# Feed-forward outputs with one 512-column product for the high and low activations

## What is computed

```python
def _swiglu(h, w_in, w_out):
    a, b = jnp.split(h @ w_in, 2, axis=-1)
    return (jax.nn.silu(a) * b) @ w_out

for layer in range(DEPTH):                      # DEPTH = 2
    x = x + 0.5 * _swiglu(_rmsnorm(x, ffn_norm[layer, 0]), ffn_w_in[layer, 0], ffn_w_out[layer, 0])
    ...                                         # hybrid mixer (layer 0), stick-breaking attention (layer 1)
    x = x + 0.5 * _swiglu(_rmsnorm(x, ffn_norm[layer, 1]), ffn_w_in[layer, 1], ffn_w_out[layer, 1])
```

## Time and profile before

| | |
|---|---|
| time, median of 3 runs | 2232.5 us (2226.9, 2232.5, 2237.2) |
| profiled execution: its own time | 2229.42 us |
| profiled execution: span of the trace | 2227.7 us |
| granted clock, mean over the span | 0.986 of full speed |
| TensorE busy with matmuls | 2143.9 us (96%) |
| VectorE busy | 1384.0 us (62%) |
| ScalarE busy | 847.6 us (38%) |
| L2002, L2003, L2004 (output stages) | 704 matmuls each, 287, 283 and 283 ns mean |
| L2499, L2500 (merged form, second block) | 256 matmuls each, 394 and 277 ns |
| L1210 and L1213 (evacuation) | 32 each, 419 and 426 ns |
| output stages, from first to last matmul start | about 157, 503, 710 and 1058 us on, some 70 us each |

### The profile page before, as it was taken

One profiled execution on the slowest core, in us unless ns is written; L12 is line 12 of the kernel. 1 busy time (PEld: TensorE's weight loads), 2 busy tenths in 40 slices (PEclk: granted clock), 3 DMA queues, 4 the chain that ended last, 5 costly groups with the idle time before them and its releaser, 6 DMA issues.

```text
span 2227.7 us, 43246 instructions
## 1 busy us (share of the span) xinstructions
PE 2143.9 (96%) x17274; PEld 1878.6 (84%) x17274; DVE 1384.0 (62%) x2303; ACT 847.6 (38%) x1336; POOL 28.9 (1%) x58
## 2 busy tenths in 40 slices
PE   7999999999999999899999999999999999999998
PEld 7999878999999998899986676788888876559987
DVE  6666657666666677766664556674355355657854
ACT  4444634444444444444531444421111233334332
POOL 0000000000000000000000000000000000000000
PEclk9999999999999999999999999999999999989999
DMA  7665424665666552466641110222222222003544
GB/s 269 245 228 185 167 75 175 241 238 183 240 237 224 198 182 99 167 229 246 226 176 38 39 39 20 102 76 94 94 95 94 95 95 95 1 19 120 182 174 147
DMA packets 50229, 325.73 MB, mean 146 GB/s; under 512 B 5328, under 2 KB 8656, under 8 KB 16976
## 3 DMA queue, kind: packets, MB, share of 16 engines
q1 hardware_dynamic: 42480, 266.62, 33.7%
q0 software_dynamic: 7648, 57.71, 6.9%
HBM read 323.26 MB, written 1.05 MB: 146 GB/s over the span
## 4 chain that ended last, share of the span: by engine, by line
PE 84%; DVE 9%; ACT 4%; issue 2%; DMA 0%; ACTq 0%; DVEq 0%; SPq 0%
PE psum L1914 17%; PE psum L1915 16%; PE psum L1916 16%; PE psum L2002 4%; PE psum L2003 4%; PE psum L2004 4%; PE psum L2499 3%; DVE w_lo L1062 2%; PE psum L2023 2%; PE psum L2338 2%; PE psum L2500 1%; ACT scratch L866 1%; ACT w_hi L620 1%; PE psum L2358 1%; PE psum L2321 1%
## 5 line engine op out<-in xcount | busy, mean ns | idle before, releaser
L1062 DVE TENSOR_TENSOR w_lo<-raw,w_hi 128x1024 fp32r<-128x1024 f32 (+1 forms) x534 | 590.2, 1146 | 229.3 <-ACT w_hi L620 215.3
L620 ACT ACTIVATE w_hi<-raw 128x1024 fp32r<-128x1024 f32 (+1 forms) x542 | 514.6, 991 | 572.3 <-PE psum L1916 351.6
L1914 PE MATMUL psum<-h_hi,w_hi 128*128 128x256 f32 (+1 forms) x2136 | 641.6, 300 | 12.8 <-DVE w_lo L1062 6.4
L1915 PE MATMUL psum<-h_lo,w_hi 128*128 128x256 f32 (+1 forms) x2136 | 633.5, 297 | 0.0
L1916 PE MATMUL psum<-h_hi,w_lo 128*128 128x256 f32 (+1 forms) x2136 | 633.1, 296 | 0.0
L1914 PEld LDWEIGHTS psum<-h_hi,w_hi 128*128 128x128 f32 x2136 | 410.1, 192 | 32.7 <-issue 12.8
L1916 PEld LDWEIGHTS psum<-h_hi,w_lo 128*128 128x128 f32 x2136 | 410.5, 192 | 10.1
L1915 PEld LDWEIGHTS psum<-h_lo,w_hi 128*128 128x128 f32 x2136 | 410.5, 192 | 9.8
L2002 PE MATMUL psum<-g_both,w_hi 128*128 128x256 f32 x704 | 202.2, 287 | 3.6 <-DVE w_lo L1062 3.6
L2003 PE MATMUL psum<-g_both,w_hi 128*128 128x256 f32 x704 | 199.3, 283 | 0.0
L2004 PE MATMUL psum<-g_both,w_lo 128*128 128x256 f32 x704 | 199.3, 283 | 0.0
(11 more groups left out here) (349 smaller groups left out, 3250.1 us busy)
## 6 DMA issues: line engine op xcount, KB each, us to landing
raw<-in_weights SPq DMA_DIRECT2D x207, 1024.0 KB, 4.8
raw_ada<-in_ada POOLq DMA_DIRECT2D x48, 1024.0 KB, 6.9
raw<-in_weights SPq DMA_DIRECT2D x64, 704.0 KB, 4.1
arena<-in_rpb POOLq DMA_DIRECT2D x1, 2048.0 KB, 10.9
arena<-in_fox_c POOLq DMA_DIRECT2D x1, 1696.0 KB, 9.2
const_region<-in_latent_c POOLq DMA_DIRECT2D x1, 1394.0 KB, 6.8
const_region<-in_even_c POOLq DMA_DIRECT2D x1, 1360.0 KB, 8.1
x_res<-in_x_lat SPq DMA_DIRECT2D x4, 256.0 KB, 7.1
```

Of the source, the lines that this page charges most:

```text
L620: nc.scalar.activation(wh[s][:, a], raw[s][:, a], ACT.Copy).then_inc(hi_ready, 1)
L1062: V.tensor_tensor(wl[s][:, a], raw[s][:, a], wh[s][:, a].bitcast(F32), ALU.subtract).then_inc(lo_ready, 1)
L1914: mm(out, sh, mh, start=n == 0, stop=False)
L1915: mm(out, sh, ml, start=False, stop=False)
```

## The change

In the output stages of the four feed-forward parts, the two matmuls of weight high become one of 512 columns: its moving operand is `g_both[:, :, g0:g0 + T]`, 256 high and then 256 low activations. Its result fills the whole bank: columns 0 to 255 get weight high times high, columns 256 to 511 weight high times low. The matmul of weight low adds to the first 256 columns only. The sum of the two halves is then formed by VectorE: a copy of the second half into `n_add`, an addition of the first half, and only then the scaling, now from `n_add` to `n_add`.

```diff
@@ -1207,9 +1207,11 @@
                     if q % 2:
                         c = q // 2
                         dve.wait_ge(gemm_done, pos.e + q + 1)
-                        V.scalar_tensor_tensor(n_add, psum[:, (pos.u + c) % 2, 0:T], 0.25, n_inv, ALU.mult,
-                                               ALU.mult).then_inc(bank_free, 1)
+                        b = (pos.u + c) % 2
+                        step(V.tensor_copy(n_add, psum[:, b, T:TJ]))
+                        V.tensor_tensor(n_add, psum[:, b, 0:T], n_add, ALU.add).then_inc(bank_free, 1)
                         freed(pos.u + c)
+                        step(V.scalar_tensor_tensor(n_add, n_add, 0.25, n_inv, ALU.mult, ALU.mult))
                         V.tensor_tensor(x[:, c, 0:T], x[:, c, 0:T], n_add, ALU.add).then_inc(x_new, 1)
                         dve.wait_ge(x_new, pos.n("xn", 1))
                         if gain:
@@ -1993,15 +1995,14 @@
                     half = j % 2
                     if half == 0:
                         bank(pos.u + 2 * i + j // 2)
-                    out = psum[:, (pos.u + j // 2) % 2, 0:T]
+                    out = psum[:, (pos.u + j // 2) % 2, :]
                     for k in range(FH):
                         a, g0 = k * P, (half * FH + k) * T
                         first, last = half == 0 and k == 0, half == 1 and k == FH - 1
                         if isinstance(i, int) and j == 1:
                             pe.wait_ge(g_ready, gb + FH + k + 1)
-                        mm(out, wh[s][:, a:a + P], gh[:, g0:g0 + T], start=first, stop=False)
-                        mm(out, wh[s][:, a:a + P], gl[:, g0:g0 + T], start=False, stop=False)
-                        ins = mm(out, wl[s][:, a:a + P], gh[:, g0:g0 + T], start=False, stop=last)
+                        mm(out, wh[s][:, a:a + P], g_both[:, :, g0:g0 + T], start=first, stop=False)
+                        ins = mm(out[:, 0:T], wl[s][:, a:a + P], gh[:, g0:g0 + T], start=False, stop=last)
                     ins.then_inc(gemm_done, 1)
```

## The result

| | before | with the change |
|---|---|---|
| time, median | 2237.1 us (5 runs, 2226.9 to 2239.1) | 2256.0 us (5 runs, 2248.6 to 2258.8) |
| profiled execution, span | 2227.7 us | 2254.6 us |
| granted clock, mean | 0.986 | 0.985 |
| VectorE busy | 1384.0 us | 1411.5 us |

The kernel became slower: ratio 1.0084, 95% interval 1.0063 to 1.0105, which is +19 us (14 to 23). The forecast was 2250 (2239 to 2259), or +18 by its sum. In a second set of runs the ratio was 1.0094 (1.0073 to 1.0115).

What follows compares the result with a forecast made beforehand. The prediction took TensorE and VectorE to be in balance in the output stages, each bounding one panel of a pair. 15.3 + 1.0 + 1.7 = +18.0 on 2229.4 gave 2247.4, plus 3.1 for the median: 2250 us (2239 to 2259).

Steps and rivals of the forecast that it cites:

- What bounds the kernel: Output stages: TensorE and VectorE in balance, each bounding one panel of a pair; TensorE stands still 0.15 us awaiting `w_lo`.
- Part 1, the merged matmul: TensorE, output stages: a block takes 0.3475 us against 0.36, saving 12.5 ns a block, 8.8 us over 704 blocks.
- Part 2, VectorE: VectorE's evacuation in the output stages: copy and addition are new, scaling costs nothing more; each evacuation grows by 0.92 us.
- d: Growth of one VectorE evacuation: 0.46 + 0.46 = 0.92 us, with ends of 0.79 and 1.0.
- Part 3, f = 0 to 2: First three output stages: pairs of panels go from 8.16 to 8.94 us; +5.1 us a stage, +15.3 for three.
- Part 4, f = 3: Fourth output stage, with looser pairs: stalls of 3.04 us, less 2.06 from shorter panels, +1.0 us.
- Part 5, behind the stages: Behind the output stages: later last evacuations cost +0.8 us after f = 0, nothing after f = 1 and 2, +0.9 after f = 3.
- The sum: Whole kernel: 15.3 + 1.0 + 1.7 = +18.0 us.
- The first (addition hidden, saving in full): Change from even to odd panel: VectorE's addition is hidden, TensorE's saving counts in full, 2224 us; chance 0.05.
- The second (part of the stall absorbed): VectorE's evacuation: copy and addition overlap or waits are free, growth near 0.6 us, +9, 2241 us; chance 0.1.
- The third (the clock): First three output stages: TensorE's standstills lower its clock; +8 us, so 2258, or +25 to +30; chance 0.08.
- The fourth (a second wait): Pairs of panels: transfers or ScalarE end behind VectorE, 0.2 to 0.4 us in each of 21, 2254 to 2258; chance 0.07.

Runs made afterwards that it cites:

- the order alone: Kernel before, with only `w_lo` of the next odd panel made earlier and ScalarE's square later, in the first three output stages: 2229.0 us, ratio 0.9986.
- the merged matmul alone: The change, but VectorE evacuates with one instruction as before and leaves out the bank's second half: 2231.5 us, ratio 0.9983 to before.
- VectorE's part alone: Kernel before with its three 256-column matmuls, plus two extra VectorE instructions of the change's kinds in each evacuation: 2259.5 us, ratio 1.0109.
- the change in three stages with the new order: The change for f = 0, 1 and 2 only, with `w_lo` ahead of the evacuation's rest; f = 3 as before: 2224.2 us, ratio 0.9965 to before.
- the copy made twice: The change with VectorE's copy of the bank's second half executed twice: 2272.2 us, ratio 1.0165 to before.
- the change with `w_lo` ahead: The change, with the next odd panel's `w_lo` made right after copy and addition, and ScalarE's square later: 2231.3 us, ratio 0.9985 to before.

## Why the prediction was right, and where its terms were off

**What bounds the kernel.** Right, and shown: the order alone brings all periods to 7.92. The shortening of TensorE's stream alone (the merged matmul alone) gave next to nothing, and VectorE's part alone gave the whole loss. The reading that foretold it was the 0.15 us of standing still between two panels, in a stage where TensorE is busy for 98.6% of the time.

**Part 1, the merged matmul.** The form is right, the size was taken from one stage and varies. In the profiled trace of the change a block steps by 0.3515 to 0.3535, in that of the change in three stages with the new order by 0.347. So the saving in the trace of the change was about 7.5 ns a block in place of 12.5. That accounts for the period of 9.02 in place of 8.94: 0.06 us on the odd panel, and some hundredths in reading.

**Part 2, VectorE.** d = 0.92 was right: steps of 0.46, a copy from PSUM at 425 ns, where copies within SBUF take 288. The choice between the two rows of copies was the one that counted.

**Part 3, f = 0 to 2.** Foretold +5.1 each from the start, or +5.24 between the first and last evacuation; measured +5.7 to +5.8. The step of 0.353 explains 0.4 of the missing half microsecond.

**Part 4, f = 3.** Foretold +1.0 (+1.1 between first and last evacuation), measured +2.2. The term was too small by half. The stalls with their restarts add up to about what was listed, 3.2 in place of 3.04, but not each in its place: panel 3 cost 0.64 where 0.24 was listed, and panel 13 cost 0.54 where 0.70 was; panel 5 cost nothing, as foretold. The shorter block gave back less (7.5 ns instead of 12.5 over 15 panels: 0.8 us), and the last evacuation came later. In the profile it starts 0.67 after the last matmul's start, where it was 0.32: the larger `w_lo` of the next stage and the work for the second block's norm end only at 1152.1, right ahead of it, which I had not followed.

**Part 5, behind the stages.** +0.8, 0, 0 and +0.9 were foretold and measured. What was missing is the clock: the same +0.9, with the late evacuation, stretched a standstill of 1.9 us to 3.2, and the granted clock fell behind it: +2.8 in one trace and +1.5 in the other, at some distance from every edited line. No term of the sum stood for it.

**The sum.** 18.0 foretold. The two measurements give 19 and 21, and the stretches that the change touches 24 in the profiled execution with the clock's part and 21 without. The median of 2256 lies inside the range, in its upper half. That +18 and +19 lie so close is partly luck. In the profile the terms that were foretold came to 21, three too few in parts 3 and 4, and the clock's part on top was in no term; the runs (+14 to +23) can't tell 18 from 21.

**The rivals.** The first (addition hidden, saving in full) fell with VectorE's part alone and with the merged matmul alone. The second (part of the stall absorbed) fell with the copy made twice. The third (the clock) did not happen where I put it: the clock is 1.00 in all output stages, even with standstills of 1.5 us in every pair. It did happen behind the last stage. Its price was put too high there: where the clock is 0.50 a 256-column matmul starts 0.213 us after the last one instead of 0.12, so a panel of before would take 3.1 us more, not 3.8. The fourth (a second wait) has no sign in the periods: with VectorE's part alone they are 9.08, the sum without any other wait.

**What stays open.** Why the same merged form steps by 0.347 in some stages and 0.353 in others, even within one execution (f = 0 and 1 of the change with `w_lo` ahead) or in two executions of one kernel (the last feed-forward part). Why the clock fell after a standstill of 3.17 us and not after one of 3.12. Also whether an addition could do without the copy; no such kernel was run.

## What to carry to other kernels

Where two engines are in balance, look at each hand-over separately: what is saved on the engine that is ahead turns into waiting, and what is added to the other is paid nearly in full. Before adding an instruction to an evacuation, look what stands behind it in that engine's program; here the order of reading the bank, then making what the next panel needs, then doing the rest took the standstills from panel 3 on out of three stages and, with the fourth left as before, turned about +20 us into -8. In the fourth stage, where other work waited behind the evacuation, the same order gained nothing. A matmul's duration in a profile isn't its price in a stream: three of 283 ns against 394 + 277 promised 125 us, the starts showed 9 at most.

## What the runs showed of the hardware

- Standstills of TensorE of 1.0 to 1.5 us, once in every 9 us, left the granted clock at 1.00 through three stages. Behind the last stage a standstill of 3.17 us was followed by a fall to the lower level in two traces, one of 3.12 us (VectorE's part alone) by none, those of 3.63 us (the copy made twice) and 3.86 us (`w_lo` ahead) by a fall again. One of 1.91 us (before) was followed by none. The fall cost 1.5 us three times and 2.8 us once, where the longer wait itself had cost 0.9 in the change. So a wait for another engine can cost more behind it than where it lies, and not in each version of a kernel.
- At a granted clock of 0.50 a 256-column matmul starts 0.213 us after the last one, at 1.00 it is 0.12.
- After a standstill the first matmul's step to the next is longer by 0.10 us (0.22 against 0.12 with 256 columns after 0.15 us, 0.34 against 0.235 with 512 after 0.98).
- The merged block of 512 and 256 columns steps by 0.347 or 0.353 us, with no difference in the program: 88.73 or 90.43 us for the same 256 blocks in two executions of the changed kernel.
